# A cast moved to ScalarE, a row of factors summed earlier, and attention scores in twos, in a two-block transformer kernel

## The reference

```python
# first block (once)
h = rmsnorm(x, g_mix) * (1 + scale1) + shift1
... # two attentions (8 heads each), gated and merged
x = x + gate1 * (merged @ w_out)
h2 = rmsnorm(x, g_ffn) * (1 + scale2) + shift2
u = depthwise_conv_seq(h2 @ w_up, conv_w, conv_b)      # 3 taps along the tokens, 5632 channels
u_val, u_gate = split(u, 2)
x = x + gate2 * ((gelu(u_gate) * u_val) @ w_down)      # 2816 -> 1024
x = rmsnorm(x, g_final)
# second kind of layer (twice): swiglu, token mixer, swiglu
# the token mixer has 24 heads: 8 "moba", 8 stick-breaking ("sb"), 8 "mla"
# stick-breaking, per head, causal mask k < q:
z = q @ k.T * scale
log_1m = where(mask, log_sigmoid(-z), 0)
suffix = reverse_cumsum(log_1m) - log_1m
w = where(mask, exp(log_sigmoid(z) + suffix), 0);  o = w @ v
```

## Time and profile before

| | |
|---|---|
| median of 3 runs | 1755.56 us (1752.27 to 1755.82) |
| profiled execution, own time | 1753.67 us |
| its span | 1751.9 us |
| mean granted clock of TensorE | 0.998 |
| TensorE (PE) busy | 1683.1 us, 96% |
| VectorE (DVE) busy | 1265.3 us, 72% |
| ScalarE (ACT) busy | 868.2 us, 50% |
| HBM read | 395.92 MB, 227 GB/s over the span |

### The profile page before, as it was taken

One profiled execution on the slowest core, in us unless ns is written; L12 is line 12 of the kernel. 1 busy time (PEld: TensorE's weight loads), 2 busy tenths in 40 slices (PEclk: granted clock), 3 DMA queues, 4 the chain that ended last, 5 costly groups with the idle time before them and its releaser, 6 DMA issues.

```text
span 1751.9 us, 29656 instructions
## 1 busy us (share of the span) xinstructions
PE 1683.1 (96%) x12356; PEld 1559.9 (89%) x12356; DVE 1265.3 (72%) x1835; ACT 868.2 (50%) x1219; POOL 21.8 (1%) x39
## 2 busy tenths in 40 slices
PE   2999999998999999999999999999999999999998
PEld 2999889987999889988989998999889989989996
DVE  6777879978787666676768775777666666768653
ACT  4555465553533364666463444544365665474332
POOL 0000000000000000000000000000000000000000
PEclk9999999999999999999999999999999999999999
DMA  9878646558587954755647786677744745537452
GB/s 384 311 255 240 252 165 219 219 203 349 187 287 285 288 184 171 200 181 207 227 141 280 281 232 257 216 289 280 289 166 169 215 180 202 209 146 273 180 181 110
DMA packets 70934, 398.93 MB, mean 228 GB/s; under 512 B 8208, under 2 KB 8464, under 8 KB 36112
## 3 DMA queue, kind: packets, MB, share of 16 engines
q1 hardware_dynamic: 67392, 386.06, 62.3%
q0 software_dynamic: 2976, 9.47, 1.6%
q10 hardware_dynamic: 432, 1.50, 0.2%
HBM read 395.92 MB, written 1.08 MB: 227 GB/s over the span
## 4 chain that ended last, share of the span: by engine, by line
PE 81%; DVE 5%; DVEq 4%; ACT 3%; DMA 3%; issue 2%; ACTq 1%; SPq 1%
PE lin L420 17%; PE lin L421 17%; PE lin L422 17%; PE att L555 17%; DVEq L1486 3%; PE att L654 3%; DMA ada_w<-in_ada 2%; PE lin L458 2%; PE lin L460 2%; PE lin L468 1%; PE pt L681 1%; DVEq L1482 1%; DVE work L1483 1%; PE att L704 1%; DMA raw<-in_w 1%
## 5 line engine op out<-in xcount | busy, mean ns | idle before, releaser
L1159 DVE TENSOR_TENSOR lo<-raw,hi 128x2048 fp32r<-128x2048 f32 x262 | 599.7, 2290 | 282.6 <-ACT hi L803 282.4
L420 PE MATMUL lin<-h_hi,hi 128*128 128x256 f32 x2480 | 700.9, 283 | 6.8 <-DVE work L1483 6.8
L421 PE MATMUL lin<-h_lo,hi 128*128 128x256 f32 x2480 | 692.7, 279 | 0.0
L422 PE MATMUL lin<-h_hi,lo 128*128 128x256 f32 x2480 | 691.4, 279 | 0.0
L803 ACT ACTIVATE hi<-raw 128x2048 fp32r<-128x2048 f32 x262 | 500.8, 1912 | 215.0 <-PE att L555 125.1
L420 PEld LDWEIGHTS lin<-h_hi,hi 128*128 128x128 f32 x2480 | 466.1, 188 | 10.1 <-issue 9.8
L421 PEld LDWEIGHTS lin<-h_lo,hi 128*128 128x128 f32 x2480 | 466.3, 188 | 1.1 <-issue 1.0
L422 PEld LDWEIGHTS lin<-h_hi,lo 128*128 128x128 f32 x2480 | 466.1, 188 | 0.0
L1175 DVE CUSTOM_DVE_ANT_0 ada_w<-ada_w,cs 128x1024 f32<-128x1024 f32 x179 | 217.8, 1218 | 24.4 <-DMA ada_w<-in_ada 24.2
L1019 ACT ACTIVATE work<-lin 128x256 f32<-128x256 f32 x88 | 33.8, 384 | 282.3 <-PE lin L422 273.9
L555 PE MATMUL att<-hi,act_hi 128*128 128x512 f32 x440 | 136.6, 392 | 3.7 <-DVE lo L1159 3.7
(11 more groups left out here) (253 smaller groups left out, 2017.5 us busy)
## 6 DMA issues: line engine op xcount, KB each, us to landing
raw<-in_w SPq DMA_DIRECT2D x269, 1024.0 KB, 4.8
ada_w<-in_ada SPq DMA_DIRECT2D x179, 512.0 KB, 5.4
ada_s<-in_ada SPq DMA_DIRECT2D x13, 512.0 KB, 16.5
bias<-in_bias POOLq DMA_DIRECT2D x16, 256.0 KB, 4.7
ffn_row<-rows POOLq DMA_DIRECT2D x5, 512.0 KB, 9.4
x<-in_x ACTq DMA_DIRECT2D x1, 1024.0 KB, 6.9
dcon<-in_dcon SPq DMA_DIRECT2D x1, 1024.0 KB, 7.5
ra<-rows POOLq DMA_DIRECT2D x2, 512.0 KB, 5.2
```

The lines of the kernel that those rows point to most:

```text
L420: mm(out, w_hi, a_hi, start=start, stop=False, skip_group_check=skip)
L421: mm(out, w_hi, a_lo, start=False, stop=False, skip_group_check=skip)
L422: return mm(out, w_lo, a_hi, start=False, stop=stop, skip_group_check=skip)
L1159: tt(lo[c % SPLIT][:], raw[:, c % RAW, :], hi[c % SPLIT][:].bitcast(F32), ALU.subtract).then_inc(*s_lo.up(c))
```

## The change

Three edits. In the convolution stage VectorE's cast to `act_hi` goes away: ScalarE makes it, for chunk k-1, between its middle taps of chunk k and its split (`act_first`), after a new signal `s_glu` from VectorE's product; VectorE makes `act_lo` of chunk k-1 after its split in chunk k (`act_second`), after a new signal `s_act_hi`. The last of each comes after the loop. The row "down" is summed in VectorE's chunk 15, not after chunk 21. In the mixers the `sb` heads are scored in twos at even steps like the others, and they use three banks in turn, the two of `att` and `pt`.

```diff
+        FIRST_SB = MIX_HEADS.index(("sb", 0))
+        def score_bank(heads, s):
+            if heads[s][0] == "sb":
+                return (att[:, 0, :], att[:, 1, :], pt[:])[(s - FIRST_SB) % 3]
+            return att[:, s % 2, :]
...
 # TensorE, scores()
-                    if s >= 2:
+                    if kind == "sb" and s >= FIRST_SB + 3:
+                        eng.wait_ge(*s_d.at((l, s - 3)))
+                    elif kind == "sb" and s == FIRST_SB + 2:
+                        eng.wait_ge(*s_pt_copied.at((l, FIRST_SB - 1)))
+                    elif s >= 2:
                         eng.wait_ge(*(s_d if heads[s - 2][0] == "sb" else s_maxed).at((l, s - 2)))
-                    bank = att[:, s % 2, :]
+                    bank = score_bank(heads, s)
...
 # TensorE, mixing()
-                        pair = s % 2 == 0 and heads[s][0] != "sb" and (s == 0 or heads[s - 1][0] != "sb")
+                        pair = s % 2 == 0 and (s == 0 or heads[s - 1][0] != "sb" or heads[s][0] == "sb")
...
 # ScalarE, convolution stage
+            def act_first(k):
+                eng.wait_ge(*s_glu.at(k))
+                act(act_hi[:, k, :], work[2 + k % 2][:, SEQ:2 * SEQ], ACT.Copy).then_inc(*s_act_hi.up(k))
...
                 ins.then_inc(*s_conved.up(k))
+                if k:
+                    act_first(k - 1)
                 split(c + SPLIT)
...
             act(cs[:], cs[:], ACT.Silu).then_inc(*s_silu.up(1))
+            act_first(FT - 1)
             log_exp()
             down("o.down")
...
 # VectorE, conv_glu(k)
                 split(c + SPLIT)
+                if k:
+                    act_second(k - 1)
                 ve.drain()
                 eng.wait_ge(*s_gated.at(("o.up", k)))
                 w = work[2 + k % 2]
-                tt(w[:, SEQ:2 * SEQ], w[:, 0:SEQ], work[k % 2][:, 0:SEQ], ALU.mult)
-                ve.drain()
-                second_of(k, "o.down", w[:, SEQ:2 * SEQ])
+                tt(w[:, SEQ:2 * SEQ], w[:, 0:SEQ], work[k % 2][:, 0:SEQ], ALU.mult).then_inc(*s_glu.up(k))
                 ada(c)
+            def act_second(k):
+                eng.wait_ge(*s_act_hi.at(k))
+                tt(act_lo[:, k, :], work[2 + k % 2][:, SEQ:2 * SEQ], act_hi[:, k, :].bitcast(F32),
+                   ALU.subtract).then_inc(*s_act.up(("o.down", k)))
...
             for k in range(FT):
                 conv_glu(k)
-            gate_of(40, "down")
+                if k == 15:
+                    gate_of(40, "down")
+            act_second(FT - 1)
```

More of the change, by code:

```diff
@@ L256, in program @@
         s_squared, s_r, s_h_hi, s_part_a = signal("squared"), signal("r"), signal("h_hi"), signal("part_a")
-        s_whole = signal("whole")
+        s_whole, s_act_hi = signal("whole"), signal("act_hi")
         s_exped, s_pt_copied, s_logged, s_w = signal("exped"), signal("pt_copied"), signal("logged"), signal("w")
@@ L266, in program @@
         s_z, s_scaled, s_h_hi_v = signal("z"), signal("scaled"), signal("h_hi_v")
+        s_glu = signal("glu")
         s_act, s_taps, s_merged, s_rot, s_lat = (signal("act_made"), signal("taps"), signal("merged"), signal("rot"),
@@ L953, in exps @@
                     w = w[:, 0:TRI]
-                    act(w, att[:, s % 2, 0:TRI], ACT.Abs)
+                    act(w, score_bank(heads, s)[:, 0:TRI], ACT.Abs)
                     nc.scalar.drain()
@@ L1336, in normed, with softplus @@
                 ins.then_inc(*s_normed.up((l, s)))
-            def softplus(l, s):
+            def softplus(l, heads, s):
                 eng.wait_ge(*s_logged.at((l, s)))
                 w = work[s % 2]
-                stt(w[:, 0:TRI], att[:, s % 2, 0:TRI], 0.0, w[:, 0:TRI], ALU.max, ALU.add)
+                stt(w[:, 0:TRI], score_bank(heads, s)[:, 0:TRI], 0.0, w[:, 0:TRI], ALU.max, ALU.add)
                 ve.drain()
@@ L1345, in softplus, with log_weights @@
                 tt(diagonal, diagonal, over(dcon[:, DCOL["sb_mul"]], 2), ALU.mult).then_inc(*s_sp.up((l, s)))
-            def log_weights(l, s):
+            def log_weights(l, heads, s):
                 eng.wait_ge(*s_turned.at((l, s)))
-                tt(work[2 + s % 2][:, 0:TRI], att[:, s % 2, 0:TRI], dcon[:, DCOL["sb_add"]], ALU.add).then_inc(
+                tt(work[2 + s % 2][:, 0:TRI], score_bank(heads, s)[:, 0:TRI], dcon[:, DCOL["sb_add"]], ALU.add).then_inc(
                     *s_d.up((l, s)))
@@ L1442, in mixing @@
                     if 0 < s <= n and heads[s - 1][0] == "sb":
-                        log_weights(l, s - 1)
+                        log_weights(l, heads, s - 1)
                     if s < n and heads[s][0] != "sb":
@@ L1447, in mixing @@
                     if s < n and heads[s][0] == "sb":
-                        softplus(l, s)
+                        softplus(l, heads, s)
                     for f in extra.get(s, []):
```

## The result

| | median, us | runs | profiled execution, us | span, us |
|---|---|---|---|---|
| before | 1754.26 | 1752.27 to 1755.82 | 1753.67 | 1751.9 |
| after | 1740.58 | 1737.84 to 1741.92 | 1739.8 | 1738.0 |

The ratio is 0.9924 [0.9912, 0.9937]: the change saves 13.3 us, between 11.0 and 15.4. The forecast was 17.8 us and 1736.5 us; the time lies 4 us above the named one and inside the range. (The median of before is 1754.26 with a fourth run, beside the three of 1755.56 above.)

The account below looks back on a forecast made before the run. TensorE, busy nearly the whole span, was taken to bound the kernel. Terms 4.6 + 5.2 + 1.5 + 6.5 = 17.8 us off the profiled 1753.67 gave 1735.9, named as 1736.5 us; range for 8 in 10: 1730 to 1745.

Parts of the forecast that it names:

- The cast, 4.6: Convolution stage: VectorE without the cast takes 11.53 us a pair of chunks, 0.58 less, over eight pairs: 4.6 us.
- the loop through ScalarE: Convolution stage: product, ScalarE's copy and split, then VectorE's split and act_lo take 5.45 us, setting chunks without ada.
- The row moved, 5.2: Down stage: the earlier row write takes the traffic gap and 1 MB of loads out of this stage, saving 5.2 us.
- the round-robin rule: DMA engines go round queues packet by packet, so the gap would stay in the down stage; sum 11.1 us.
- the gap: Head of the down stage: 2.5 us without DMA traffic after the row's write, moving with it to the convolution stage.
- The end of the down stage, 1.5: End of the down stage: VectorE reaches the second half's product less late; 3.3 us at most, 1.5 taken.
- the `ada` ring: Down stage: reloading ada buffers loops in 5.4 us a chunk, just under TensorE's 5.48, leaving VectorE about 2 us late.
- The pairs, 6.5: Mixers: two sb heads scored together cost 0.85 us like one, eight pairs giving 6.8 us, 6.5 taken.
- Rival B: Convolution stage not bound by the loop through ScalarE, VectorE in time at the down stage's end: 23.2 us, 1731; chance 0.10.
- rival C: Mixers: score pairs bring nothing, hidden by VectorE or not overlapped on TensorE: 11.3 us saved, 1743; chance 0.09.
- rival D: Convolution stage: the moved gap starves it and stops TensorE; 1758 us if a load lands 41 us after the write; chance 0.05.
- Rival A: Down stage gives nothing back, through another cause of the gap or the `ada` ring: 11.1 us saved, 1743; chance 0.14.

Follow-up runs that it names:

- y1: The changed kernel with ScalarE's split placed ahead of its copy to act_hi in each chunk; 1737.25 us, 0.9894 of the kernel before.
- x1: The kernel before with only the cast moved to ScalarE and act_lo deferred; 1750.86 us, 0.9982, and 1748.42 us in a second, single execution.
- x3: The kernel before with only the sb scores in twos on three banks; 1748.64 us, 0.9972 of the kernel before.
- x5: The kernel before with the cast moved and the row summed after chunk 15, sb heads still single; 1746.35 us, 0.9956 of the kernel before.
- x2: The kernel before with only the row "down" summed after chunk 15; 1748.44 us, 0.9974 of the kernel before.
- x4: The kernel before with the row "down" written in 32-byte instead of 4-byte pieces, its numbers in wrong places; 1750.51 us, 0.9981 of the kernel before.
- y3: The changed kernel with ScalarE evicting the latent products in the middle of mixer steps 13 and 14; 1740.83 us, 0.9910 of the kernel before.
- y2: The changed kernel with one ada block per down-stage chunk put off to the next chunk; 1738.31 us, 0.9898 of the kernel before.
- y4: The changed kernel with the edits of y1, y2 and y3 together; 1732.82 us, 0.9867, and 1730.59 us, 0.9868 in the repeat.

## Why the prediction was right, and where not

*What bounds.* Right. TensorE's stops of the earlier trace rows were what could be had; all three parts gave time, and they add up within their intervals (3.2, 4.6 and 4.9 alone, 13.3 together).

*The cast, 4.6.* The mechanism is right: 11.53 us a pair, and y1 shows by taking the order of copy and split apart that the loop through ScalarE sets it. The stage gave 5.3 to 5.6 because the pair before was on average 97.56 / 8 = 12.20 us, where the prediction added up 12.11 from the earlier trace rows and so counted 0.58 for 0.67: six of the eight pairs took 12.11, two took 12.46. Which chunk holds the wait came out the other way round (4.95 and 6.58). What stays open is why the time of this part alone shows only 3.2 us (1.6 to 4.7). Two things are seen to take some of it back: the two waits of 0.28 us outside the stage, and the down stage, which in both profiles of x1 is longer than before (69.54 and 66.75 against 65.84). With the way behind it x1 has 84.62 and 81.69 against 81.13 before and 82.23 in x3; and with the row early, x5 has 80.16 against 77.68 in x2. But the two profiles of x1 themselves lie 2.9 us apart in that column, so it is not shown that a faster convolution stage costs the down stage time.

*The row moved, 5.2.* The path is right, against the round-robin rule: the gap went with the write, in the changed kernel and in x2, and x4 shows what makes it. The size came out in three of six profiles, and that the first profile of after was one of them is luck: the stage gave 5.45 in the first profile of after, 4.94 in x2 and 5.4 in y1, but 0.5 in the second profile of after, 0.4 in x5 and 2.9 in y3, where the ring made the stops that the gap had made. By time, x2 gives 4.6 (2.8 to 6.3). The spare time in the convolution stage was 4 us by the forecast; the one wait of 0.52 us says it was used up.

*The end of the down stage, 1.5.* This is the term that failed. The prediction knew the `ada` ring (a loop of 5.4 us a chunk against TensorE's 5.48) and took VectorE to come out some 2 us late. It comes out 1.5 to 5.1 us late, 3.4 in the mean of six profiles, before 3.5: nothing gained. The size that it had wrong is the 6.3 us from the end of the product that frees a buffer to the use of the next block in it. Before, it was 6.0 to 7.0 us for the five blocks behind the gap; in the six profiles with the early row and the old ring the blocks that VectorE waited for took 7.1 us in the mean (5.1 to 8.2). With 7.1 the same loop is 7.1 + 1.1 + 2.2 + 1.1 = 11.5 us, 5.75 a chunk and over TensorE's 5.48 (an estimate from these rows). In the timeline above the block's wait of 2.49 us stands right in front of the split: whatever `ada` waits, the split waits too, and the product with the row stands behind both. Why the loads take longer stays open. Stage and way together gave 82.4 - 77.7 = 4.7 us where 5.2 + 1.5 = 6.7 were forecast. y2 relaxes the ring and has 75.02, 2.7 less than that mean and 1.0 less than the lowest of the six; y4 with the same edit has 73.25 and 71.06. No stop in the stage is left in any of the three, so that the ring is the reason is shown; how much of the 2.7 is scatter of the clock behind it (8.53 us of way in y2, 5.57 to 7.26 in y4) is not.

*The pairs, 6.5.* The overlap on TensorE is right: two heads in 0.86 us. In each layer 4 x 0.85 = 3.4 us leave TensorE, and 1.8 to 2.4 us of it arrive. Of the loss, 1.4 us in layer 0 and 1.0 in layer 1 in the first profile, 1.1 and 0.8 are the new stops (0.79 and 0.30; in layer 1 only 0.79); the rest was not followed. The prediction looked for the risk at VectorE and at the score banks; it came at ScalarE, which evicts the latent products last in its step. y3 moved that and got the mixers to 2.7 and 3.1 below before; the wait for VectorE (L1410) grew to 0.71 in its place. Term and measured: 6.5, and 4.3 and 4.1 in the two profiles of after, 4.9 (3.0 to 6.7) by time.

Rival B (loop doesn't bind) fails by y1, rival C by the pairs' 0.86 us and x3's gain, and rival D because TensorE does not stop for the moved gap. Rival A held in part: the second profile of after (65.36 us) and x5 (65.45) have the stops of the `ada` ring at the full price that the gap had, so its chance of 0.14 was not too high, and its price should have been put on the sum as a share.

## What to carry to other kernels

When a stop goes on the engine that bounds, the engine that feeds it has to be followed to the end of the stage: what it still waits for decides whether the gain arrives or waits at the next hand-over. Where two steps stand in one queue, put the one whose inputs are always there ahead of the one that waits for another engine (y1: 1.6 us for two lines in the other order). And a prefetch ring whose loop is estimated within some per cent of the pace it must keep is to be counted as a stop, or its uses put one place later (y2).

## What the runs showed of the hardware

A write of 1024 pieces of 4 bytes, 4 KB in all, holds up nearly all traffic of the core's 16 DMA engines, beginning 3 to 5 us after its issue. GpSimd waits 9.4 us for it before and 11.3 us in the changed kernel; the windows have 66 GB/s or less from 377 to 385 us before, and 23 to 43 GB/s from 342.5 to 350 us after. For the same 4 KB in pieces of 32 bytes (x4) it waits 2.9 us, and the traffic is low for 3 us (0 to 103 GB/s) and back at 410 GB/s by 380 us. The Trainium skill, "DMA: Bandwidth & Descriptors", section "Queues, rings and completion order", says that an engine goes round its queues packet by packet; the traces do not agree with that alone, as SP's queue moved almost nothing meanwhile.

TensorE has two paces at a granted clock of 1.00 that differ by 1%. The same stretch of x1 in its two profiles, without any stop (windows of 60 us: busy time, instructions):

```profile
950.00:1010.00 60.00, 60.00 (x512) 60.00 (x511) 47.72 (x66) 23.64 (x22) 0.00 (x0) 1.00 0.75 277
```

```profile
948.00:1008.00 60.00, 60.00 (x517) 60.00 (x516) 47.80 (x67) 24.09 (x22) 0.00 (x0) 1.00 0.77 281
```

512 products against 517. In the first 125 us of that stretch the lag grows evenly to 1.17 us and then stays, where products of 512 columns follow. Before has the same 1.17 us against after in its last stretch (191.44 and 190.24 us) and once more between the mixers (382.54 and 381.70 us, where the longer wait of 0.28 us hides part of it), so 2.3 of the 13.9 us between the two profiles are not the change's. The fourteen profiles have four such stretches each, and 12 of the 56 are longer by 1.1 to 1.2 us in this way. What sets the pace I did not find out; it is why the sums above are made by stage.
